# A two-layer hybrid decoder trunk: the last gate item behind the first half's branches, the first half's merged rows turned by VectorE and transfers, and a value product moved

## The chip, the core and the metric

The kernel runs on one core of a Trainium2 chip. The time is the device time of one execution in microseconds (us). Engines are TensorE (PE), VectorE (DVE), ScalarE (ACT), GpSimd (POOL) and the queue of SyncE (SP), which issues the transfers.

## What is computed

For each of two layers, on x of 256 rows and 1024 columns in float32 (cut from the reference):

```python
h = rms_norm(x)
proj = h @ w_in                    # pool | diff q,k,v | stick-breaking | forgetting | 4 x 1024 gate logits
gates = sigmoid(g_logit.reshape(b, s, 4, 1024) + b_gate)
merged = 0
for n, o in enumerate((o_pool, o_diff, o_sb, o_fox)):
    merged = merged + gates[:, :, n] * (o @ w_branch[rows of branch n])
x = x + merged @ w_out
x = x + swiglu(rms_norm(x))
```

The differential attention (four heads) and the forgetting attention, "fox" (four heads, taken as two pairs), are softmax attentions: scores, softmax, then probabilities times values.

## The kernel before

**Work and its units.** All weight matrices are streamed once per layer. A list `ITEMS` (L48 to L69) cuts them into items of 512 columns, and `plan_units` cuts the items into 144 units per layer, each of two blocks of 128 rows of the weights. An item's result is 2 x 128 rows by 512 columns and lies in one half of the PSUM tensor `bulk`; items take the two halves in turn, so an item may start only when the item two before it has been read out (`released_by`). Each weight is split into a rounded high part and the rest (`w_hi` by ScalarE, `w_lo` by VectorE), and so is each left operand; one block is three products (L1761, L1762, L1765), so a unit is 12 products of 512 columns (2 blocks x 2 row tiles x 3).

**Order of the items in a layer.** Seven items of the mixers (units 0 to 27), eight of the gates (28 to 59), then for each half j of the columns the four branches (1, 2, 1 and 1 units: 60 to 64 and 65 to 69), then `out` (70 to 77), then the feed-forward items from 78 on. Gate item g holds the logits of branch g // 2, half g % 2.

**The order around the items** is written out by hand. Each engine has a table from a slot to stages: TensorE's `MIXING_PE` says what it does ahead of unit "slot", `MIXING_ACT` and `MIXING_DVE` what ScalarE and VectorE do in their turn of the loop over units. In each turn these two run the slot's stages in the order of the table and then prepare the weights four units ahead (`split_hi`, L812, and `split_lo`, L1087). `split_hi` waits until the unit five before its own is done, which ties both engines to TensorE. VectorE's products of a branch (`branch`, L1388, gate times result) come after the table's stages of the same slot. Every engine works in order: what waits holds what is behind it.

**Attention stages.** For a head h: `scores` (TensorE, into banks A and B), `maxima` (VectorE, L1302 to L1305), `softmax` (exponentials by ScalarE, L968 to L970; scaling by VectorE), `tr_probs` (TensorE turns the probabilities, bank T, L1673), `probs_evac` (ScalarE copies them, `probsT`, L976), `pv` (TensorE, value product into bank O, L1683 to L1685) and `pv_evac` (VectorE copies it to `o_d`, L1338). Before TensorE writes a bank it waits for the last reader of that bank, in `take`:

```python
def pv(layer, kind, h):
    pe.wait_ge(probsT_ready, nth(probsT_ready, layer, (kind, h)))
    if kind == "diff":
        pe.wait_ge(v_ready, nth(v_ready, layer, ("dv", 1)))
        take("O", o_d_ready, layer, h)
```

**Turning rows.** Left operands must lie turned. The merged rows are turned by TensorE (`tr_merged`, L1703, four transposes for each row tile) into banks A and B for the first half and T and O for the second, then split by ScalarE (L816) and VectorE (L1094). The fox rows, the differential rows and the feed-forward activations go another way: VectorE transposes 32 x 32 blocks (`turn_blocks`, L1419) and transfers put the blocks in place, for the first two by way of DRAM (`rows_to_dram`, `rows_from_dram`), for the activations from SBUF to SBUF in four groups of four transfers (L690). SP issues such a group behind the weight load of its unit, and loads the weights six units ahead, each when its buffer is free.

**Merging.** GpSimd adds the four gated branches of a half (L784, six additions a half), in place in `wide`, once VectorE's products are there (`gated`), and signals `merged_ready`.

## Time and profile before

| | |
|---|---|
| median of 3 runs | 849.31 us (849.13 to 849.34) |
| the profiled execution | 849.36 us, its span 847.6 us |
| TensorE busy | 842.3 us (99%) |
| VectorE busy | 605.3 us (71%) |
| ScalarE busy | 445.5 us (53%) |
| GpSimd busy | 114.9 us (14%) |

A busy share is an average over the whole span. The timeline gives each instruction's start and length; in the chain of waits each piece is what the piece behind it waited for. "sb" and "wide" are SBUF tensors, "bank..." and "bulk" lie in PSUM.

### The profile page before, as it was taken

The numbers are of one execution on the slowest core, as the hardware profiler recorded it, in microseconds if no ns is written. First come the engines' busy times: TensorE is split into PE (matmuls) and PEld (weight loads), VectorE is DVE, ScalarE is ACT, GpSimd is POOL, SyncE is SP. The second block draws the span as 40 slices with busy tenths as digits, with TensorE's granted clock in tenths as the row PEclk, the third lists the DMA queues.
The fourth block names the chain that finished last, engine by engine and source line by source line (L and its number), as shares of the span: only waits on it lengthen the run. The fifth ranks groups of instructions, "written<-read, shape, count | busy, mean of one in ns | idle before, by whom it ended". The sixth has DMA issues, their size and how long they took to land.

```text
span 847.6 us, 11122 instructions
## 1 busy us (share of the span) xinstructions
PE 842.3 (99%) x4126; PEld 699.2 (83%) x4126; DVE 605.3 (71%) x890; ACT 445.5 (53%) x650; POOL 114.9 (14%) x89
## 2 busy tenths in 40 slices
PE   9999999999999999999999999999999999999998
PEld 7888888888888888888888888888888888888887
DVE  7885977679677666665479668868687776666643
ACT  6657645754454455444365675557543644444431
POOL 0750201004502000000005402010054000000000
PEclk9999999999999999999999999999999999999999
DMA  9846666477567777666566365764965577666651
GB/s 340 286 164 179 200 214 192 148 243 232 184 199 244 203 220 218 202 218 217 173 185 191 109 191 172 237 202 123 296 189 169 177 236 205 205 202 220 222 188 50
DMA packets 100934, 170.43 MB, mean 201 GB/s; under 512 B 12944, under 2 KB 26768, under 8 KB 100880
## 3 DMA queue, kind: packets, MB, share of 16 engines
q1 hardware_dynamic: 100448, 169.07, 63.8%
q8 instruction: 33, 0.54, 0.3%
q10 hardware_dynamic: 432, 0.66, 0.3%
q14 instruction: 21, 0.17, 0.1%
HBM read 160.77 MB, written 3.15 MB: 193 GB/s over the span
## 4 chain that ended last, share of the span: by engine, by line
PE 99%; DMA 1%; ACT 0%; issue 0%; DVE 0%; ACTq 0%
PE bulk L1761 30%; PE bulk L1765 30%; PE bulk L1762 30%; PE bankAB L1526 2%; DMA raw<-in_w_in_dram 1%; PE bankT L1673 0%; PE bulk L1808 0%; PE bankAB L1662 0%; PE bulk L1789 0%; PE bankAB L1620 0%; PE bulk L1795 0%; PE bankAB L1535 0%; PE bankO L1631 0%; PE bankO L1683 0%; PE bankO L1691 0%; PE bankO L1685 0%
## 5 line engine op out<-in xcount | busy, mean ns | idle before, releaser
L1087 DVE TENSOR_TENSOR w_lo<-raw,w_hi 128x1024 fp32r<-128x1024 f32 (+1 forms) x288 | 360.2, 1268 | 116.9 <-ACT w_hi L812 114.4
L812 ACT ACTIVATE w_hi<-raw 128x1024 fp32r<-128x1024 f32 (+1 forms) x286 | 295.5, 1047 | 206.7 <-PE bulk L1765 202.6
L1761 PE MATMUL bulk<-w_hi,hT_hi 128*128 128x512 f32 (+1 forms) x880 | 342.8, 390 | 0.0
L1762 PE MATMUL bulk<-w_lo,hT_hi 128*128 128x512 f32 (+1 forms) x880 | 339.3, 386 | 0.0
L1765 PE MATMUL bulk<-w_hi,hT_lo 128*128 128x512 f32 (+1 forms) x880 | 336.3, 386 | 0.0
L1761 PEld LDWEIGHTS bulk<-w_hi,hT_hi 128*128 128x128 f32 x880 | 165.3, 188 | 33.1 <-issue 0.5
L1765 PEld LDWEIGHTS bulk<-w_hi,hT_lo 128*128 128x128 f32 x880 | 165.0, 188 | 33.3
L1762 PEld LDWEIGHTS bulk<-w_lo,hT_hi 128*128 128x128 f32 x880 | 165.4, 188 | 32.0
L1761 PE MATMUL bulk<-w_hi,aT_hi 128*128 128x512 f32 x174 | 67.8, 390 | 0.0
L1765 PE MATMUL bulk<-w_hi,aT_lo 128*128 128x512 f32 x174 | 67.7, 389 | 0.0
L1762 PE MATMUL bulk<-w_lo,aT_hi 128*128 128x512 f32 x174 | 67.7, 389 | 0.0
L784 POOL TENSOR_TENSOR wide<-wide 128x512 f32<-128x512 f32 x24 | 44.2, 1860 | 117.1 <-DVE wide L1388 116.6
L1094 DVE TENSOR_TENSOR aT_lo<-wide,aT_hi 128x512 fp32r<-128x512 f32 (+1 forms) x24 | 14.5, 644 | 38.4 <-ACT aT_hi L816 38.4
L750 POOL TENSOR_TENSOR wide<-wide,ropeA 128x512 f32<-128x512 f32 x8 | 13.4, 1679 | 198.0 <-DVE wide L1190 197.9
L1761 PEld LDWEIGHTS bulk<-w_hi,aT_hi 128*128 128x128 f32 x174 | 32.7, 188 | 6.8
L1765 PEld LDWEIGHTS bulk<-w_hi,aT_lo 128*128 128x128 f32 x174 | 32.7, 188 | 6.8
L1762 PEld LDWEIGHTS bulk<-w_lo,aT_hi 128*128 128x128 f32 x174 | 32.7, 188 | 6.7
L816 ACT ACTIVATE aT_hi<-wide 128x512 fp32r<-128x512 f32 (+1 forms) x24 | 13.0, 589 | 45.9 <-DMA wide<-wide 45.9
L1761 PE MATMUL bulk<-w_hi,oT_hi 128*128 128x512 f32 x80 | 31.3, 391 | 0.0
L1765 PE MATMUL bulk<-w_hi,oT_lo 128*128 128x512 f32 x80 | 31.1, 389 | 0.0
L1762 PE MATMUL bulk<-w_lo,oT_hi 128*128 128x512 f32 x80 | 31.1, 389 | 0.0
L1011 ACT ACTIVATE wide<-bulk,y_ffn 128x512 f32<-128x512 f32 (+1 forms) x24 | 14.3, 650 | 18.2 <-PE bulk L1765 16.0
(239 smaller groups left out, 715.6 us busy)
## 6 DMA issues: line engine op xcount, KB each, us to landing
raw<-in_w_in_dram SPq DMA_DIRECT2D x110, 512.0 KB, 4.5
raw<-in_w_ffn_up_dram SPq DMA_DIRECT2D x80, 512.0 KB, 4.1
raw<-in_w_ffn_down_dram SPq DMA_DIRECT2D x44, 512.0 KB, 3.6
raw<-in_w_branch_dram SPq DMA_DIRECT2D x20, 512.0 KB, 5.3
raw<-in_w_out_dram SPq DMA_DIRECT2D x16, 512.0 KB, 3.3
wide<-wide SPq DMA_DIRECT2D x160, 32.0 KB, 2.7
bias<-in_b_gate_dram SPq DMA_DIRECT2D x16, 256.0 KB, 4.9
raw<-in_w_ffn_up_dram SPq DMA_DIRECT2D x16, 256.0 KB, 3.4
```

The source lines that it names most:

```text
L750: pool.tensor_tensor(ta, x, ropeA[:, i, t:t + 1, :].broadcast_to([P, 8, HD]), ALU.mult)
L784: ins = pool.tensor_tensor(m, m, wide[:, t, n * D + j * NC:n * D + (j + 1) * NC], ALU.add)
L812: act.activation(w_hi[:, g % RING, :, 0:width], raw[:, g % RAW, :, 0:width], ACT.Copy).then_inc(hi_ready, 1)
L816: ins = act.activation(dst, src, ACT.Copy) if scale is None else act.activation(dst, src, ACT.Copy, scale=scale)
L1011: act.activation(ff_tmp(t, p, width), item_bank(layer, ITEM_AT[item], t)[:, 0:width], ACT.Sigmoid, scale=y_ffn[:, t:t + 1]).then_inc(ff_si ...
L1087: vec.tensor_tensor(w_lo[:, g % RING, :, 0:width], raw[:, g % RAW, :, 0:width], w_hi[:, g % RING, :, 0:width].bitcast(F32), ALU.subtract). ...
L1094: ins = vec.tensor_tensor(dst, src, high.bitcast(F32), ALU.subtract)
L1526: ins = pe.matmul(dst, a[a_part], b[b_part], start=start and a_part + b_part == 0, stop=stop and a_part == 1, skip_group_check=True)
L1761: pe.matmul(dst, hi, whi, start=(k == ks[0]), stop=False)
L1762: pe.matmul(dst, hi, wlo, start=False, stop=False)
L1765: ins = pe.matmul(dst, lo, whi, start=False, stop=(k == ks[-1] or g == DEPTH * U - 2 and i == 1 and t == 1))
```

## The change

- The item of gate 7 (the gate of branch 3, second half) stands behind the four branches of the first half. The units are now: gates 0 to 6 at 28 to 55, first half's branches at 56 to 60, gate 7 at 61 to 64, second half's branches at 65 to 69 as before.
- The sigmoid of branch 3 is taken in two halves (`sigmoid_last`).
- The first half's merged rows are no longer turned by TensorE: VectorE turns them (stage `turn` "merged", slot 63), sixteen transfers from SBUF to SBUF in the queue at units 67 to 70 put them in place, and the split reads them from there in slot 68. Before, it read the banks in slot 69. The differential rows are turned in slot 48 instead of 49.
- The value product of differential head 2 moves on TensorE from slot 39 to slot 42, ahead of the transposes of head 3; its copy by VectorE moves from slot 39 to slot 42. `tr_forget` and `forget_evac` move from slot 39 to 37.

```diff
@@ -59,10 +59,11 @@
     ("dv", "w_in", [(OFF["dv"], 512)], KD),
     ("pf", "w_in", [(OFF["u"], 256), (OFF["f"], 4)], KD),
 ]
-ITEMS += [(("gate", g), "w_in", [(OFF["gate"] + g * NC, NC)], KD) for g in range(8)]
+GATES = [(("gate", g), "w_in", [(OFF["gate"] + g * NC, NC)], KD) for g in range(8)]

 KB = [range(0, 2), range(2, 6), range(6, 8), range(8, 10)]
-ITEMS += [(("branch", j, n), "w_branch", [(j * NC, NC)], KB[n]) for j in range(2) for n in range(4)]
+ITEMS += GATES[:7] + [(("branch", 0, n), "w_branch", [(0, NC)], KB[n]) for n in range(4)]
+ITEMS += GATES[7:] + [(("branch", 1, n), "w_branch", [(NC, NC)], KB[n]) for n in range(4)]
 ITEMS += [(("out", j), "w_out", [(j * NC, NC)], KD) for j in range(2)]
 NPAIR = 5
 for _p in range(NPAIR):
@@ -133,10 +134,10 @@
...
-    (37, "scores", "diff", 3), (37, "pv", "diff", 1), (39, "tr_probs", "diff", 2), (39, "pv", "diff", 2), (39, "tr_forget"), (42, "tr_probs", "diff", 3), (42, "scores", "fox", 0), (42, "pv", "diff", 3),
-    (52, "tr_probs", "fox", 1), (56, "pv", "fox", 1), (68, "tr_merged", 0),
-    (73, "tr_merged", 1)]
+    (37, "scores", "diff", 3), (37, "pv", "diff", 1), (37, "tr_forget"), (39, "tr_probs", "diff", 2), (42, "pv", "diff", 2),
+    (42, "tr_probs", "diff", 3), (42, "scores", "fox", 0), (42, "pv", "diff", 3), (47, "tr_probs", "fox", 0),
+    (56, "pv", "fox", 1), (73, "tr_merged", 1)]
...
@@ -173,7 +174,7 @@
     if stage == "pv":
         return [((stage, *args), "O")]
     if stage == "tr_merged":
-        return [((stage, args[0], t), ("AB", "TO")[args[0]][t]) for t in range(TT)]
+        return [((stage, args[0], t), "TO"[t]) for t in range(TT)]
     raise ValueError(stage)


@@ -189,9 +190,12 @@
 FF_BLOCKS = [4] * NPAIR + [2]
 FF_DONE = [FIRST[("ffu", _p)] + 4 for _p in range(NPAIR)] + [LAST["fflast"] + 1]
 FF_TURN = [_u + 1 for _u in FF_DONE[:-1]] + [FF_DONE[-1] + 4]
-TURN_AT = {"fox": 33, "diff": 49}
+TURN_AT = {"fox": 33, "diff": 48, "merged": 63}
 SPREAD_AT = {}
 BY_DRAM = ('fox', 'diff')
+for _s in ('merged',):
+    for _a in range(NQUAD):
+        SPREAD_AT.setdefault(TURN_AT[_s] + AHEAD + _a, []).append((_s, _a))
 for _s in ('fox', 'diff'):
     for _a, _way in enumerate(("out", "back")):
         SPREAD_AT.setdefault(TURN_AT[_s] + AHEAD + _a, []).append((_s, _way))
@@ -210,13 +214,13 @@
...
-    (36, "softmax", "diff", 2), (37, "probs_evac", "diff", 1), (38, "softmax", "diff", 3), (38, "probs_evac", "diff", 2),
+    (36, "softmax", "diff", 2), (37, "probs_evac", "diff", 1), (37, "forget_evac"), (38, "softmax", "diff", 3),
-    (55, "diff_evac", 0), (56, "pv_evac", "fox", 1), (60, "sigmoid", 3, 0), (61, "sigmoid", 3, 1), (69, "merged_evac", 0),
+    (49, "pool_evac_b"), (52, "probs_evac", "fox", 1), (53, "sigmoid", 2, 0), (53, "sigmoid", 2, 1), (55, "diff_evac", 1),
+    (55, "diff_evac", 0), (56, "pv_evac", "fox", 1), (57, "sigmoid_last", 0, 0), (57, "sigmoid_last", 0, 1),
+    (65, "sigmoid_last", 1, 0), (66, "sigmoid_last", 1, 1), (68, "merged_evac", 0), (72, "merged_evac", 1)]
...
@@ -225,11 +229,11 @@
...
-    (39, "pv_evac", "diff", 2), (39, "softmax", "diff", 3), (39, "fox_evac", "fq"), (39, "fox_evac", "fk"), (40, "gate", 2),
-    (41, "maxima", "fox", 0), (41, "softmax", "fox", 0), (42, "pv_evac", "diff", 3), (44, "gate", 3), (47, "maxima", "fox", 1),
-    (48, "diff_norm"), (48, "pv_evac", "fox", 0), (49, "softmax", "fox", 1), (49, "gate", 4), (49, "pool_evac_b"),
-    (49, "turn", "diff"), (52, "gate", 5), (55, "diff_evac", 1), (55, "diff_evac", 0), (56, "gate", 6),
-    (57, "pv_evac", "fox", 1), (60, "gate", 7), (69, "merged_evac", 0), (71, "merged_evac", 1)]
+    (39, "softmax", "diff", 3), (39, "fox_evac", "fq"), (39, "fox_evac", "fk"), (40, "gate", 2), (41, "maxima", "fox", 0),
+    (41, "softmax", "fox", 0), (42, "pv_evac", "diff", 2), (42, "pv_evac", "diff", 3), (44, "gate", 3),
+    (47, "maxima", "fox", 1), (48, "diff_norm"), (48, "pv_evac", "fox", 0), (48, "turn", "diff"), (49, "softmax", "fox", 1),
+    (49, "gate", 4), (49, "pool_evac_b"), (52, "gate", 5), (55, "diff_evac", 1), (55, "diff_evac", 0), (56, "gate", 6),
+    (57, "pv_evac", "fox", 1), (63, "turn", "merged"), (65, "gate", 7), (68, "merged_evac", 0), (71, "merged_evac", 1)]
...
@@ -457,7 +461,7 @@

             kind = stage if isinstance(stage, str) else stage[0]
             blocks = FF_BLOCKS[stage[1]] if kind == "act" else 4
-            return (*{"act": normed_place, "dq": late, "diff": late}.get(kind, early), blocks)
+            return (*{"act": normed_place, "diff": late, "merged": late}.get(kind, early), blocks)

         def spread_columns(stage, t, blocks):

@@ -545,7 +549,7 @@
         lam_exp = signal("lam_exp", ["exp"])
         lam_sum = signal("lam_sum", ["sum", "lam"])
         gate_ready = signal("gate_ready", [(g, t) for g in range(8) for t in range(TT)])
-        gate_open = signal("gate_open", [(n, t) for n in range(4) for t in range(TT)])
+        gate_open = signal("gate_open", [(n, t) for n in range(3) for t in range(TT)] + [(3, j, t) for j in range(2) for t in range(TT)])
         gated = signal("gated", [(j, n, t) for j in range(2) for n in range(4) for t in range(TT)])
         summed = signal("summed", [(j, n) for j in range(2) for n in (1, 2)])
         merged_ready = signal("merged_ready", [(j, t) for j in range(2) for t in range(TT)])
@@ -992,11 +996,21 @@
                 g = wide[:, t, n * D:(n + 1) * D]
                 act.activation(g, g, ACT.Sigmoid).then_inc(gate_open, 1)

+            def sigmoid_last(layer, j, t):
+                act.wait_ge(gate_ready, nth(gate_ready, layer, (6 + j, t)))
+                g = wide[:, t, 3 * D + j * NC:3 * D + (j + 1) * NC]
+                act.activation(g, g, ACT.Sigmoid).then_inc(gate_open, 1)
+
             def merged_evac(layer, j):
+                if j == 0:
+                    wait_spread(act, layer, "merged")
+                    for t in range(TT):
+                        lhs_part(layer, ("merged", 0, t), by_quads(hT[0], (0, 4), t), spread_columns("merged", t, (0, 4)))
+                    return
                 for t in range(TT):
                     act.wait_ge(stage_done, nth(stage_done, layer, ("tr_merged", j, t)))
                     lhs_part(layer, ("merged", j, t), hT[0][:, 4 * j:4 * j + 4, t * P:(t + 1) * P],
-                             bank[("AB", "TO")[j][t]].rearrange("p (k q) -> p k q", k=4))
+                             bank["TO"[t]].rearrange("p (k q) -> p k q", k=4))

             def ff_gate(layer, p):
                 item, width = (("ffg", p), NC) if p < NPAIR else ("fflast", 256)
@@ -1383,14 +1397,18 @@

                 for t in range(TT):
                     wait_item(vec, layer, ("branch", j, n), t)
-                    vec.wait_ge(gate_open, nth(gate_open, layer, (n, t)))
+                    vec.wait_ge(gate_open, nth(gate_open, layer, (n, t) if n < 3 else (n, j, t)))
                     g = wide[:, t, n * D + j * NC:n * D + (j + 1) * NC]
                     vec.tensor_tensor(g, item_bank(layer, ITEM_AT[("branch", j, n)], t), g, ALU.mult).then_inc(gated, 1)

             def merged_evac(layer, j):
                 for t in range(TT):
+                    if j == 0:
+                        lhs_rest(layer, ("merged", 0, t), by_quads(hT[1], (0, 4), t), spread_columns("merged", t, (0, 4)),
+                                 by_quads(hT[0], (0, 4), t))
+                        continue
                     lhs_rest(layer, ("merged", j, t), hT[1][:, 4 * j:4 * j + 4, t * P:(t + 1) * P],
-                             bank[("AB", "TO")[j][t]].rearrange("p (k q) -> p k q", k=4),
+                             bank["TO"[t]].rearrange("p (k q) -> p k q", k=4),
                              hT[0][:, 4 * j:4 * j + 4, t * P:(t + 1) * P])

             def ff_gate(layer, p):
@@ -1426,6 +1444,8 @@
                     turn_blocks(layer, stage, *(rotated, ("fk", 1)), lambda t: fox_gained[:, t, :])
                 elif stage == "diff":
                     turn_blocks(layer, stage, *(o_normed, "normed"), lambda t: o_d[:, t, :, :].rearrange("p h d -> p (h d)"))
+                elif stage == "merged":
+                    turn_blocks(layer, stage, *(merged_ready, (0, 1)), lambda t: merged(t)[:, 0:NC])

             def act_turn(layer, p):

@@ -1697,7 +1717,7 @@
             def tr_merged(layer, j):
                 for t in range(TT):
                     pe.wait_ge(merged_ready, nth(merged_ready, layer, (j, t)))
-                    name = ("AB", "TO")[j][t]
+                    name = "TO"[t]
                     take(name, lhs_lo, layer, ("merged", j, t))
                     for k in range(4):
                         ins = pe.transpose(bank[name][:, k * P:(k + 1) * P], merged(t)[:, (4 * j + k) * P:(4 * j + k + 1) * P], identity)
```


**TensorE, slot 39 before.** Transposes of head 2's probabilities, its value product (L1683 to L1685), and the transposes of the forget rows (L1554):

```order
L1673 MATMUL bankT<-con,probs_diff 128x128 [waits probsT_ready,probs_ready]
L1673 MATMUL bankT<-con,probs_diff 128x128 x2
L1683 MATMUL bankO<-v_d,probsT 128x128 [waits o_d_ready,v_ready,probsT_ready]
L1684 MATMUL bankO<-v_d,probsT 128x128
L1685 MATMUL bankO<-v_d,probsT 128x128
L1554 MATMUL bankT<-con,forget_rows 128x128 [waits probsT_ready,forget_out]
L1554 MATMUL bankT<-con,forget_rows 128x128 x3
```

The last two pieces leave this slot: the forget rows go to slot 37, the value product to slot 42, which now begins with it, head 3's transposes and the fox scores (lines of the changed file stand 20 further on):

```order
L1703 MATMUL bankO<-v_d,probsT 128x128 [waits o_d_ready,v_ready,probsT_ready]
L1704 MATMUL bankO<-v_d,probsT 128x128
L1705 MATMUL bankO<-v_d,probsT 128x128
L1693 MATMUL bankT<-con,probs_diff 128x128 [waits probsT_ready,probs_ready]
L1693 MATMUL bankT<-con,probs_diff 128x128 x2
L1546 MATMUL bankAB<-keys_hi,queries_hi 128x256 [waits forgetsT_ready,exped,qkT_ready,masks_ready]
L1546 MATMUL bankAB<-keys_hi,queries_hi 128x256
```

and ends with the last scores and head 3's value product, which waits for `o_d_ready`, as it did:

```order
L1674 MATMUL bankAB<-keys_hi,queries_hi 128x256 x2
L1677 MATMUL bankAB<-keys_hi,queries_hi 128x128 x2
L1682 MATMUL bankAB<-masks 128x256 x2
L1703 MATMUL bankO<-v_d,probsT 128x128 [waits o_d_ready,v_ready,probsT_ready]
L1704 MATMUL bankO<-v_d,probsT 128x128
L1705 MATMUL bankO<-v_d,probsT 128x128
```

Slot 42 so holds two value products into bank O, where it held one.

**VectorE, slots 41 and 42.** Before: the fox maxima and softmax, the low part for unit 45, one copy of a value product (head 3's):

```order
L1087 TENSOR_TENSOR w_lo<-raw,w_hi 128x1024 [waits hi_ready]
L1302 TENSOR_REDUCE row_max<-bankAB 128x2 [waits stage_done]
L1303 TENSOR_REDUCE row_max<-bankAB 128x2
L1305 TENSOR_SCALAR nmx<-row_max 128x4 [waits vec_step]
L1315 RECIPROCAL inverse<-den 128x4 [waits stage_done,exped]
L1330 TENSOR_SCALAR sb<-sb,inverse 128x256 [waits vec_step]
L1331 TENSOR_SCALAR sb<-sb,inverse 128x128
L1330 TENSOR_SCALAR sb<-sb,inverse 128x256
L1331 TENSOR_SCALAR sb<-sb,inverse 128x128
L1087 TENSOR_TENSOR w_lo<-raw,w_hi 128x1024 [waits hi_ready]
L1338 COPY o_d<-bankO 128x2x128 [waits stage_done]
```

In the change the same rows end with both copies, head 2's and head 3's, in one place (lines 14 further on); the copy of head 2 stood in slot 39, ahead of head 3's softmax:

```order
L1329 RECIPROCAL inverse<-den 128x4 [waits stage_done,exped]
L1344 TENSOR_SCALAR sb<-sb,inverse 128x256 [waits vec_step]
L1345 TENSOR_SCALAR sb<-sb,inverse 128x128
L1344 TENSOR_SCALAR sb<-sb,inverse 128x256
L1345 TENSOR_SCALAR sb<-sb,inverse 128x128
L1101 TENSOR_TENSOR w_lo<-raw,w_hi 128x1024 [waits hi_ready]
L1352 COPY o_d<-bankO 128x2x128 [waits stage_done] x2
L1101 TENSOR_TENSOR w_lo<-raw,w_hi 128x1024 [waits hi_ready] x2
```

So the copy of head 2's product has moved behind the fox maxima, the fox softmax and one low part.

**VectorE, slots 68 and 69.** Before, from the low parts of units 70 and 71: the product of branch 1 of the second half (slot 68), and behind it the split of the first half's merged rows out of bankAB (slot 69):

```order
L1087 TENSOR_TENSOR w_lo<-raw,w_hi 128x1024 [waits hi_ready] x2
L1388 TENSOR_TENSOR wide<-bulk,wide 128x512 [waits gate_open,unit_done] x2
L1087 TENSOR_TENSOR w_lo<-raw,w_hi 128x1024 [waits hi_ready]
L1094 TENSOR_TENSOR hT_lo<-bankAB,hT_hi 128x4x128 [waits lhs_hi] x2
L1388 TENSOR_TENSOR wide<-bulk,wide 128x512 [waits gate_open,unit_done] x2
L1087 TENSOR_TENSOR w_lo<-raw,w_hi 128x1024 [waits hi_ready]
```

Now, from gate 7 in slot 65: the split, out of the turned rows in `o_d`, stands in slot 68 ahead of that product:

```order
L1392 SCALAR_TENSOR_TENSOR wide<-bulk,y_attn,bias 128x512 [waits bias_loaded1,unit_done] x2
L1101 TENSOR_TENSOR w_lo<-raw,w_hi 128x1024 [waits hi_ready]
L1402 TENSOR_TENSOR wide<-bulk,wide 128x512 [waits gate_open,unit_done] x2
L1101 TENSOR_TENSOR w_lo<-raw,w_hi 128x1024 [waits hi_ready] x2
L1108 TENSOR_TENSOR hT_lo<-o_d,hT_hi 128x4x128 [waits lhs_hi] x2
L1402 TENSOR_TENSOR wide<-bulk,wide 128x512 [waits gate_open,unit_done] x2
L1101 TENSOR_TENSOR w_lo<-raw,w_hi 128x1024 [waits hi_ready]
```

The split has changed places with the product of branch 1.

## Rows read from the trace of the kernel before

**Rows 1.** The page: busy time of TensorE, its granted clock by slice, the chain's shares.
```profile
PE 842.3 (99%) x4126; PEld 699.2 (83%) x4126; DVE 605.3 (71%) x890; ACT 445.5 (53%) x650; POOL 114.9 (14%) x89
...
PEclk9999999999999999999999999999999999999999
...
PE 99%; DMA 1%; ACT 0%; issue 0%; DVE 0%; ACTq 0%
```

**Rows 2.** Who waited for whom, TensorE: us in total, times, longest.
```profile
PE bankO L1683 <- ACT probsT L976: 1.2, 2, 0.6
```

**Rows 3.** Timeline, slot 39, layer 0: start us, us, engine line operation.
```profile
123.51 0.49 PE L1673 MATMUL bankT<-con,probs_diff 128*128 128x128 f32 x3
...
124.03 0.49 ACT L976 ACTIVATE probsT<-bankT 128x384 f32<-128x384 f32 x1
...
124.58 0.49 PE L1683 MATMUL bankO<-v_d,probsT 128*128 128x128 f32 x2 [0.58 <-ACT probsT L976]
```

**Rows 4.** The chain of waits, layer 0, units 56 to 68: start us, us, what.
```profile
181.41 0.43 PE bulk L1761
...
214.32 0.87 PE bankAB L1703 x8
```

**Rows 5.** Timeline, slot 42, layer 0, TensorE, VectorE and ScalarE.
```profile
135.85 0.39 PE L1683 MATMUL bankO<-v_d,probsT 128*128 128x128 f32 x2
...
136.05 0.69 DVE L1302 TENSOR_REDUCE row_max<-bankAB 128x2 f32<-128x512 f32 x1 [2.35 <-PE bankAB L1662]
...
137.31 0.48 ACT L968 ACTIVATE sb<-bankAB,nmx 128x256 f32<-128x256 f32 x1 [1.36 <-DVE nmx L1305]
...
139.06 0.18 DVE L1315 RECIPROCAL inverse<-den 128x4 f32<-128x4 f32 x1 [1.79 <-ACT sb L970]
...
140.20 1.22 DVE L1087 TENSOR_TENSOR w_lo<-raw,w_hi 128x1024 fp32r<-128x1024 f32 x1
...
141.34 0.42 DVE L1338 COPY o_d<-bankO 128x256 f32<-128x256 f32 x1
```

**Rows 6.** Timeline, layer 0, first half's branch 1 and the additions behind it.
```profile
200.75 1.29 DVE L1388 TENSOR_TENSOR wide<-bulk,wide 128x512 f32<-128x512 f32 x2 [0.34 <-PE bulk L1765]
...
201.52 11.69 POOL L784 TENSOR_TENSOR wide<-wide 128x512 f32<-128x512 f32 x6 [55.59 <-DVE wide L1388]
```

**Rows 7.** Timeline, feed-forward part: turns, transfers and copies of two activation tiles.
```profile
269.54 1.29 DVE L1419 STREAM_TRANSPOSE wide<-wide 128x512 f32<-128x512 f32 x2
...
272.54 2.50 SPq L690 DMA_DIRECT2D wide<-wide  x4
...
281.87 3.20 SPq L690 DMA_DIRECT2D wide<-wide  x4
...
286.34 1.16 ACT L816 ACTIVATE aT_hi<-wide 128x512 fp32r<-128x512 f32 x2 [1.90 <-DMA wide<-wide]
...
287.00 1.29 DVE L1094 TENSOR_TENSOR aT_lo<-wide,aT_hi 128x512 fp32r<-128x512 f32 x2 [1.30 <-ACT aT_hi L816]
...
292.07 1.30 DVE L1419 STREAM_TRANSPOSE wide<-wide 128x512 f32<-128x512 f32 x2
...
308.17 1.16 ACT L816 ACTIVATE aT_hi<-wide 128x512 fp32r<-128x512 f32 x2 [1.97 <-DMA wide<-wide]
```

**Rows 8.** Timeline, layer 0: the turn and the landing of the differential rows.
```profile
162.04 0.42 DVE L1094 TENSOR_TENSOR oT_lo<-bankO,oT_hi 128x256 fp32r<-128x256 f32 x1 [0.88 <-ACT oT_hi L816]
...
167.36 1.29 DVE L1419 STREAM_TRANSPOSE v_d<-o_d 128x512 f32<-128x512 f32 x2
...
182.32 1.34 ACT L816 ACTIVATE oT_hi<-o_d,small 128x512 fp32r<-128x512 f32 x2 [5.03 <-DMA o_d<-rows_diff]
...
183.08 2.19 DVE L1363 SCALAR_TENSOR_TENSOR oT_lo<-o_d,small,oT_hi 128x128 fp32r<-128x128 f32 x8 [4.35 <-ACT oT_hi L816]
```

**Rows 9.** Timeline, start of the kernel: the warm-up products.
```profile
0.97 4.63 PE L1817 MATMUL bulk<-warm 128*128 128x128 bf16 x48 [0.97 <-DVE warm L1452]
...
4.83 0.78 PE L1817 MATMUL bulk<-warm 128*128 128x128 bf16 x11
```

More of the change, by code:

```diff
@@ L135 @@
     (30, "scores", "diff", 1), (30, "pv", "diff", 0), (35, "cum"), (35, "scores", "diff", 2), (35, "tr_probs", "diff", 1),
-    (37, "scores", "diff", 3), (37, "pv", "diff", 1), (39, "tr_probs", "diff", 2), (39, "pv", "diff", 2), (39, "tr_forget"), (42, "tr_probs", "diff", 3), (42, "scores", "fox", 0), (42, "pv", "diff", 3),
-    (47, "tr_probs", "fox", 0), (47, "scores", "fox", 1), (47, "pool_a"), (47, "pv", "fox", 0), (50, "pool_b"),
-    (52, "tr_probs", "fox", 1), (56, "pv", "fox", 1), (68, "tr_merged", 0),
-    (73, "tr_merged", 1)]
+    (37, "scores", "diff", 3), (37, "pv", "diff", 1), (37, "tr_forget"), (39, "tr_probs", "diff", 2), (42, "pv", "diff", 2),
+    (42, "tr_probs", "diff", 3), (42, "scores", "fox", 0), (42, "pv", "diff", 3), (47, "tr_probs", "fox", 0),
+    (47, "scores", "fox", 1), (47, "pool_a"), (47, "pv", "fox", 0), (50, "pool_b"), (52, "tr_probs", "fox", 1),
+    (56, "pv", "fox", 1), (73, "tr_merged", 1)]
 _PE = [(0, "tr_norm", "attn", 0, 1)] + MIXING_PE + [(F0, "tr_norm", "ffn", 0, 1)]
@@ L1029, in _ @@
                           diff_evac=diff_evac, gate=nothing, sigmoid=sigmoid, branch=nothing,
-                          merged_evac=merged_evac, ff_gate=ff_gate, ff_up=nothing, turn=nothing, act_turn=nothing, act_evac=act_evac)
+                          merged_evac=merged_evac, ff_gate=ff_gate, ff_up=nothing, sigmoid_last=sigmoid_last, turn=nothing, act_turn=nothing, act_evac=act_evac)
             def first_hi(k):
```

4 lines of the change are left out of this document (1 added, 3 removed).

## The prediction

> **What bounds the kernel now.** I read the page first: TensorE is busy for 842.3 of 847.6 us, and the chain of waits lies on it for 99% [rows 1]. So the time is TensorE's own work plus whatever it stands still for, and the table of who waited for whom is short: apart from the start it has one line, two waits for the turned probabilities, 1.2 us in total [rows 2]. VectorE, ScalarE, GpSimd and the queues have slack on average, but the average says nothing about one place. A change of order can win only what TensorE no longer does or waits for; it can lose as much as any single wait it makes. So after the gains I follow each piece that was moved, with its queue, in the timeline.
>
> One unit of weights (12 products) takes TensorE 2.7425 us: unit 56 starts at 181.41, slot 68 at 214.32, nothing but 12 units between them [rows 4]. The start of unit k in the timeline of before is 181.41 + (k - 56) x 2.7425. Everything is worked out for layer 0 on this time base and doubled, since both layers run the same order.
>
> **Gains.** (a) The eight transposes of the first merged half leave TensorE: 0.87 us in the chain [rows 4], per layer. Twice: -1.7. (b) In slot 39 the value product of the third differential head follows its own transposes at once and waits for ScalarE's copy. The three transposes start at 123.51, take about 0.11 apart, and something else could start at 123.84; the product starts at 124.58 [rows 3]. So 0.74 us, twice -1.5 (the table's 1.2 counts from the modelled end of the transposes). In slot 42 that copy is long done. The product itself and the four transposes of the forget rows are only moved. In slot 37 ScalarE now stands before the forget copy until TensorE has come there; the hi part queued behind it is used by VectorE some us later, so I cost that at nothing. The split last sigmoid is ScalarE work beside TensorE's, at nothing too.
>
> **First new wait, slot 42.** TensorE now does: value product 2, transposes 3, scores of the first fox pair, value product 3. Both value products write bank O, so product 3 waits until VectorE has copied product 2 out. That copy used to be in VectorE's slot 39; it now stands in slot 42, behind the fox maxima, the fox softmax and a w_lo part of slot 41 (front matter, VectorE's order). And the fox maxima wait for the scores that TensorE issues just ahead of product 3. So TensorE waits for a whole round trip that begins with its own scores. The trace has this trip, since the copy of product 3 stood at its end: maxima from 136.05, ScalarE's exponentials from 137.31, VectorE again from 139.06, the w_lo part at 140.20, the copy 141.34 to 141.76; TensorE issued product 3 at 135.85 [rows 5]. 141.76 - 135.85 = 5.91, and 0.05 for the hand-over (ScalarE ends at 124.52, TensorE starts at 124.58 [rows 3]). I take 5.96, twice +11.9. Nothing in the trip depends on what was moved, so I give it 5.5 to 6.3. What queues behind the wait is every later product of TensorE; the other engines only get ahead, and I count no gain for that.
>
> **Second new wait, unit 69.** The branches of the first half now lie four units earlier. VectorE's product of branch 1 came right after unit 62, which ended at 200.61, and GpSimd's six additions ran from 201.52 for 11.69 us, to 213.21 [rows 6]. Four units earlier is 10.97 us earlier: merged rows complete at 202.24, VectorE turns them then. From there I take the price of the same thing in the feed-forward part, with the same sixteen 32 KB transfers and four weight loads between them: VectorE's turn at 269.54, transfers issued from 272.54 to 285.07 (the last group 281.87 + 3.20), ScalarE's copy at 286.34, VectorE's subtractions 287.00 to 288.29; a second time 292.07 to 308.17 [rows 7]. So 16.1 to 16.8 us from turn to ScalarE's copy: 218.3 to 219.0, and 1.95 more until both subtractions are done: 220.3 to 221.0. In slot 68 VectorE's order has these subtractions ahead of the product of branch 1 of the second half, which is what frees the bank for the second half's branch 3, unit 69. Its first tile takes half of 1.29 [rows 6]: 220.9 to 221.6, and the hand-over. Unit 69 would start at 181.41 + 13 x 2.7425 = 217.06. Wait: 3.9 to 4.6, I take 4.3, twice +8.6. Before, nothing stood ahead of that product. The bounds are wider than these two samples: 3 if the queue of transfers, free of feed-forward traffic, lands each group sooner; 6 if GpSimd or the turn is late by a unit's half.
>
> **What stays hidden.** The differential rows are needed at unit 57 (184.15) instead of 61. Before, VectorE was through with them at 185.27 (183.08 + 2.19), 1.1 late for the new order; but their turn moves from 167.36 to right behind the fox copy that ends at 162.46 [rows 8], 4.9 earlier, and their way out one load earlier in the queue. 3.8 to spare: nothing, at most the 1.1 and a gate product behind it. The 16 added transfers hold the queue for some 0.6 us each, and the weight loads behind them run six units ahead of their use: nothing. The last transposes (slot 73) follow a POOL chain that the second wait shifts by as much as TensorE: 0 to 0.5.
>
> Sum without the clock: 849.36 (the profiled execution; the median of the runs is 849.31) - 1.7 - 1.5 + 11.9 + 8.6 = **866.7 us**.
>
> **The clock.** The 48 warm-up products of 128 columns took 4.44 us, from 0.97 to 5.41, against 48 x 0.057 = 2.7 at the pace of the units (2.7425 / 12 / 4); the last 11 lie clearly closer (0.78 us) than the rest [rows 9]. So TensorE, idle before the kernel, begins at the lower level (1.2 GHz) though the column of the granted clock prints 1.00 there, and to climb once costs 1.7 us. No row shows whether 6 us of standing still bring it back; after the start it never stood for more than 0.6 us [rows 2]. Bounds are nothing and 1.7 for each of four waits, 0 to +6.8. I take it for the two long ones and not for the two shorter: +3.4.
>
> The Trainium skill, page "TensorE: Matmul & The Clock Gate", Part 1, says that the throttled level is the default and that activity releases it, and warns against gaps between bursts of products. By that page all four waits may bring the clock down (the third rival); the start of this trace agrees with its first half, no row here bears on the second.
>
> **Forecast: 870.1 us**, 2.4% slower. 0.44.
>
> **Rivals.**
> - The clock holds: 866.7. For it: every slice of the page has the clock at full, across all the small waits [rows 1]. 0.13.
> - The clock falls at all four waits: 866.7 + 6.8 = 873.5. 0.13.
> - Only the first wait is there, since the transfers land over 4 us sooner than the feed-forward ones: 849.4 - 3.2 + 11.9 = 858.1, 861.5 with the clock. Against it: the queue issues its four groups one weight load apart, which sets 12 of the 16 us. 0.11.
> - Only the second: 854.8. It needs the copy of product 2 ahead of the fox maxima, and the order has it behind. 0.04.
> - A third wait: the differential rows land late at unit 57, or GpSimd's last additions hold the transposes of slot 73, 1 to 3.5 us per layer: 872 to 877. For it: ScalarE stood 5.0 us for this very transfer before [rows 8]. 0.10.
> - **Not slower.** Place: bank O in slot 42 and the bank of unit 69. If VectorE stands far enough ahead at both (5.96 and 4.3 us), TensorE keeps only the gains, 849.4 - 3.2 = 846.1. It decides when both waits together fall below 1.6 us per layer, the gains. Against it: the first trip starts with TensorE's own scores, so no lead of VectorE's shortens it. 0.05.
>
> **How the numbers follow.** The range reaches from the first wait alone with the clock's price (861.5, less 1.5 for the spread of its terms) to the upper end of a third wait: 860 to 877. Outside are "only the second", "not slower", the first wait alone at full clock and what lies above 877, about 0.15. Faster by over 0.2% (what a measurement of this kernel can tell from no change): 0.05. Within 0.2%: 0.01. Slower: 0.94.
>
> **What would show it.** TensorE's waits: a new line at the first value product of a differential head for VectorE's copy of o_d, some 5.8 us, twice; a new line at a bulk product for VectorE's wide, about 4 us, twice; the 1.2 us for probsT gone, the eight transposes into bankAB gone. Busy TensorE falls in share, not in us, unless the granted clock shows slices below 1 after the waits. ScalarE's first-half copy starts 16 to 17 us after the turn. Wrong would be: no wait at bank O (my reading of the order fails), a turn long before 202 on this time base, or a wait at unit 57.

## The result and the profile after

| | before | after |
|---|---|---|
| median | 849.22 us (848.98 to 849.34, 4 runs) | 877.12 us (875.34 to 877.60, 4 runs) |
| the profiled execution | 849.36 us, span 847.6 us | 875.34 us, span 873.5 us |

The change is slower: ratio 1.0325, interval 1.0307 to 1.0343. The page of the kernel after, the lines that answer to [rows 1] (granted clock by slice, in tenths, and the chain's shares):

```profile
PE 849.1 (97%) x4110; PEld 703.9 (81%) x4110; DVE 607.7 (70%) x894; ACT 445.7 (51%) x654; POOL 112.2 (13%) x89
...
PEclk9999998999899999999999999989998999999999
...
PE 95%; DVE 2%; DMA 1%; ACT 1%; SPq 1%; issue 1%; ACTq 0%; DVEq 0%
```

TensorE has 16 instructions less and is busy 6.8 us longer: the granted clock is below full in four slices. The chain of waits leaves TensorE for 5% of the span. Who was waited for, against [rows 2] (us in total, times, longest):

```profile
PE bankO L1703 <- DVE o_d L1352: 11.8, 2, 5.9
PE bulk L1781 <- DVE wide L1402: 8.7, 2, 4.8
```

The wait for probsT is gone, and there are two new lines, each twice. These are the two waits that the prediction named.

**Slot 42**, timeline of layer 0 (start us, us, engine line operation), against [rows 5]:

```profile
134.44 0.39 PE L1682 MATMUL bankAB<-masks 128*128 128x256 bf16 x2
...
134.87 0.69 DVE L1316 TENSOR_REDUCE row_max<-bankAB 128x2 f32<-128x512 f32 x1 [1.38 <-PE bankAB L1682]
...
136.13 0.47 ACT L972 ACTIVATE sb<-bankAB,nmx 128x256 f32<-128x256 f32 x1 [1.36 <-DVE nmx L1319]
...
139.02 1.22 DVE L1101 TENSOR_TENSOR w_lo<-raw,w_hi 128x1024 fp32r<-128x1024 f32 x1
140.15 0.42 DVE L1352 COPY o_d<-bankO 128x256 f32<-128x256 f32 x1
...
140.72 0.77 PE L1703 MATMUL bankO<-v_d,probsT 128*128 128x128 f32 x2 [5.88 <-DVE o_d L1352]
```

The round trip is the one read in the trace of before: scores, maxima at 134.87, exponentials at 136.13, a w_lo part at 139.02, the copy of product 2 at 140.15. The masks' two products end their turn at about 134.67; the value product starts at 140.72, 6.05 us later.

**Unit 69**, layer 0, against [rows 6, 7]:

```profile
197.32 11.57 POOL L788 TENSOR_TENSOR wide<-wide 128x512 f32<-128x512 f32 x6 [51.50 <-DVE wide L1402]
```
```profile
208.94 1.30 DVE L1437 STREAM_TRANSPOSE v_d<-wide 128x512 f32<-128x512 f32 x2 [1.19 <-POOL wide L788]
...
226.48 1.29 DVE L1108 TENSOR_TENSOR hT_lo<-o_d,hT_hi 128x512 fp32r<-128x512 f32 x2 [5.79 <-ACT hT_hi L820]
227.69 1.28 DVE L1402 TENSOR_TENSOR wide<-bulk,wide 128x512 f32<-128x512 f32 x2
```
```profile
211.79 3.41 SPq L694 DMA_DIRECT2D o_d<-v_d  x4
...
215.87 2.42 SPq L694 DMA_DIRECT2D o_d<-v_d  x4
...
218.97 2.41 SPq L694 DMA_DIRECT2D o_d<-v_d  x4
...
222.04 2.41 SPq L694 DMA_DIRECT2D o_d<-v_d  x4
```
```profile
225.82 1.15 ACT L820 ACTIVATE hT_hi<-o_d 128x512 fp32r<-128x512 f32 x2 [6.39 <-DMA o_d<-v_d]
```
```profile
228.52 0.77 PE L1781 MATMUL bulk<-w_hi,oT_hi 128*128 128x512 f32 x1 [4.81 <-DVE wide L1402]
...
661.03 0.77 PE L1781 MATMUL bulk<-w_hi,oT_hi 128*128 128x512 f32 x1 [3.90 <-DVE wide L1402]
```

From VectorE's turn to ScalarE's copy it is 16.88 us, and VectorE's subtraction stands ahead of the branch product that frees the bank. The last product before the wait started at 223.33, so the next was due at 223.56 and came at 228.52: 4.96 us. In layer 1 the idle time shown is 3.90; from start to start, counted in the same way, it is 4.06 (656.74 to 661.03, less the 0.23 of one product).

**The clock**, TensorE in three stretches around the first wait (stretch: us, busy (instructions), granted clock, DMA share, GB/s):

```profile
134.80:140.70 5.90, 0.03 (x1) 0.74 0.39 126
140.70:144.30 3.60, 3.58 (x12) 0.50 0.50 148
144.30:148.00 3.70, 3.70 (x17) 0.98 0.47 142
```

After the wait the granted clock is 0.50, the lower of the two levels (1.2 GHz), for 3.6 us, and the bulk products lie 0.427 us apart; then they lie 0.2275 apart. The same shows behind all four waits, for 3.6 and 4.4 us in layer 0, 3.9 and 5.7 in layer 1. A product of 0.427 us loses 0.20, a share of 0.467: 17.6 x 0.467 = 8.2 us. With it the profiled execution adds up: 849.36 - 3.2 (the gains as predicted) + 2 x 6.05 + 4.96 + 4.06 + 8.2 = 875.5, against 875.34.

The differential rows came in time for unit 57: VectorE's split ran from 185.04, behind 0.77 of waiting, and TensorE's table has no line for it.

### The profile page after: what moved, and what is told of

Read it like the earlier page. It is cut to its first block, busy times and chain, and to the rows that moved or that the text cites. A ratio compares the mean times of both kernels' runs of the same rounds, so it can differ in the third digit from the quotient of the medians.

```text
span 873.5 us, 11126 instructions
## 1 busy us (share of the span) xinstructions
PE 849.1 (97%) x4110; PEld 703.9 (81%) x4110; DVE 607.7 (70%) x894; ACT 445.7 (51%) x654; POOL 112.2 (13%) x89
## 4 chain that ended last, share of the span: by engine, by line
PE 95%; DVE 2%; DMA 1%; ACT 1%; SPq 1%; issue 1%; ACTq 0%; DVEq 0%
PE bulk L1781 29%; PE bulk L1782 29%; PE bulk L1785 29%; PE bankAB L1546 2%; SPq L694 1%; DMA raw<-in_w_in_dram 1%; DVE w_lo L1101 1%; PE bankT L1693 0%; PE bankAB L1682 0%; PE bulk L1828 0%; DMA o_d<-v_d 0%; PE bulk L1809 0%; PE bankAB L1640 0%; PE bulk L1815 0%; PE bankO L1703 0%
## 5 line engine op out<-in xcount | busy, mean ns | idle before, releaser
L1781 PE MATMUL bulk<-w_hi,oT_hi 128*128 128x512 f32 x80 | 33.6, 420 | 8.7 <-DVE wide L1402 8.7
L1782 PE MATMUL bulk<-w_lo,oT_hi 128*128 128x512 f32 x80 | 33.0, 412 | 0.0
L1781 PEld LDWEIGHTS bulk<-w_hi,oT_hi 128*128 128x128 f32 x80 | 16.1, 201 | 13.2 <-issue 9.8
```

Of the source, the lines that this page charges most:

```text
L1781: pe.matmul(dst, hi, whi, start=(k == ks[0]), stop=False)
L1782: pe.matmul(dst, hi, wlo, start=False, stop=False)
```

## The experiments

**Undo the first wait** (e1): VectorE copies product 2 one slot earlier, ahead of the fox maxima.

```diff
-... (41, "maxima", "fox", 0),
-    (41, "softmax", "fox", 0), (42, "pv_evac", "diff", 2), (42, "pv_evac", "diff", 3), ...
+... (41, "pv_evac", "diff", 2), (41, "maxima", "fox", 0),
+    (41, "softmax", "fox", 0), (42, "pv_evac", "diff", 3), ...
```

> The changed kernel with one entry moved: VectorE copies the third differential head's product in slot 41, ahead of the fox maxima, instead of in slot 42. Theory (both waits are real and each lowers the clock): the 5.9 us wait of TensorE at bank O goes in both layers and with it the stretches at half clock behind it (3.7 and 3.9 us of work, so 1.7 and 1.8 us lost): 877.1 - 12.0 - 3.5 = 861.6 us, TensorE's second wait stays at about 4.9 and 3.8 us. Rival (the copy only looks like the cause, and TensorE is held by something else in slot 42, such as the probabilities or bank A and B): the wait stays with another releaser, above 873 us.

Measured 858.41 us (858.13 to 858.61), ratio 1.0108 (1.0093 to 1.0123). Only the second line was left:

```profile
PE bulk L1781 <- DVE wide L1402: 8.6, 2, 4.7
```

Taking away two waits of 6.05 us gave 18.7 us, 6.6 more than the waits themselves. Between the profiled executions it is 17.2 (875.34 to 858.13), and that adds up: 12.1 of waits, 3.5 of the low stretches behind them, which go with them, and 1.4 because the two stretches that stay are 4.0 and 3.1 us long instead of 4.4 and 5.7, and cost 3.3 together instead of 4.7. So the expected 861.6 was 3.2 too high: 1.4 of that is the shorter stretches, and 1.8 that the median of the change lies above its profiled execution.

**Undo the second wait, first try** (e2): VectorE's split of the merged rows one slot later, behind the branch product.

```diff
-    ... (65, "gate", 7), (68, "merged_evac", 0), ...
+    ... (65, "gate", 7), (69, "merged_evac", 0), ...
```

> The changed kernel with one entry moved: VectorE splits the first merged half in slot 69, behind the product of branch 1 of the second half, instead of in slot 68. Theory: unit 69 no longer waits; unit 70 then waits for the split itself and for the branch product behind it, about 1.8 us, too short for the clock: 877.1 - 8.7 + 3.6 - 4.5 (clock) = 867.5 us, 865 to 869. Rival (the transfers' landing alone sets the time, wherever the split stands): the wait only moves to unit 70 and keeps 4 us or more per layer, above 874 us.

Measured 875.28 us (875.01 to 876.42), ratio 1.0312 (1.0294 to 1.0329), 1.8 below the change, and the two intervals overlap: next to none of the 9.6 us expected. The timeline of e2, VectorE and TensorE in layer 0:

```profile
221.51 1.29 DVE L1402 TENSOR_TENSOR wide<-bulk,wide 128x512 f32<-128x512 f32 x2 [0.34 <-PE bulk L1785]
228.29 1.23 DVE L1101 TENSOR_TENSOR w_lo<-raw,w_hi 128x1024 fp32r<-128x1024 f32 x1 [5.49 <-ACT w_hi L816]
229.43 1.29 DVE L1108 TENSOR_TENSOR hT_lo<-o_d,hT_hi 128x512 fp32r<-128x512 f32 x2
230.63 1.28 DVE L1402 TENSOR_TENSOR wide<-bulk,wide 128x512 f32<-128x512 f32 x2
```
```profile
231.42 0.77 PE L1781 MATMUL bulk<-w_hi,hT_hi 128*128 128x512 f32 x1 [4.51 <-DVE wide L1402]
```

The branch product at 221.51 no longer waits, but the next w_lo part waits 5.49 us for ScalarE, whose high part is stuck behind its own copy of the merged rows (started at 226.16). The wait moved one unit on. So both engines hold their queues for the transfers.

**Both moves together** (e4), the edits of e1 and e2.

> The moves of the first two experiments together. Theory: gains 3.2 us in two layers (eight transposes each, 1.7; the wait for the probabilities, 1.5), one wait of about 1.8 us left per layer at unit 70, no slice below full clock: 849.2 - 3.2 + 3.6 = 849.6 us, 848.5 to 850.5. Rival (the new places of the items cost something the two waits hid, at unit 57 or slot 73): above 851 us, with a third wait in the table.

Measured 858.86 us (858.57 to 859.01), ratio 1.0113 (1.0098 to 1.0128), the same as e1 within 0.5, and not the 849.6 expected: the second move is worth nothing with the first wait gone, either. The line of waits reads like that of e1, though the wait now stands ahead of unit 70, as in e2 (beside it there is one wait of 0.7 us in the feed-forward part of layer 1):

```profile
PE bulk L1781 <- DVE wide L1402: 8.8, 2, 4.8
```

**The waits with TensorE kept busy** (e3): 100 idle products of 128 columns into an unused part of bank T stand ahead of the value product of head 3. What the kernel computes is unchanged.

```diff
+                if (kind, h) == ("diff", 3):
+                    for _ in range(100):
+                        pe.matmul(bank["T"][:, 384:512], warm[:, :], warm[:, :], start=True, stop=True)
```

> The changed kernel with 100 idle products of TensorE (zeros into unused columns of bank T) put ahead of the value product of head 3 in both layers, inside the wait; they change no result. At the pace of full clock they fill about 5.7 of the 6.0 us. Theory (standing still lowers the clock): product 3 starts at the same time, the granted clock stays at 1.0 behind the first wait, 1.7 and 1.8 us come back: 877.1 - 3.5 = 873.6 us. Rival (what is lost behind the wait is not the clock, or idle products do not hold it): 877 us, the same slices below 1.

Measured 871.98 us (871.24 to 872.17), ratio 1.0267 (1.0251 to 1.0282), 5.1 below the change. Its second wait, and TensorE in layer 0:

```profile
PE bulk L1784 <- DVE wide L1402: 9.3, 2, 5.4
```
```profile
134.83 5.75 PE L1700 MATMUL bankT<-warm 128*128 128x128 bf16 x100
140.88 0.46 PE L1706 MATMUL bankO<-v_d,probsT 128*128 128x128 f32 x2 [0.30 <-DVE o_d L1352]
```

The value product comes as late as before, 6.05 us after the end of the masks' products, and no low stretch follows it. The waits did not get shorter, so the time is won by the clock alone, but not all of it behind the first waits. Between the profiled executions it is 4.1 us (875.34 to 871.24): 3.5 behind the first waits, as expected, and 1.3 because the stretches behind the second waits are 4.0 and 3.4 us long here instead of 4.4 and 5.7, less 0.6 for second waits that are longer (5.55 and 4.09 us from start to start). The rest of the 5.1 comes from the medians, which lie 1.8 (the change) and 0.7 (e3) above the profiled executions.

**Idle products in both waits** (e11): as e3, and 66 more ahead of unit 69.

> The changed kernel with idle products of TensorE in both waits (100 ahead of head 3's value product, 66 ahead of unit 69); nothing else is changed. Theory (waits and clock are all there is): no slice below full clock, 849.2 - 3.2 + 12.0 + 8.7 = 866.7 us, plus what the waits measured between starts add, up to 868. Rival (the clock costs less than the 8 to 10 us that are unexplained by the waits): above 870 us with the clock at full.

Measured 869.82 us (869.78 to 871.42), ratio 1.0234 (1.0211 to 1.0257), 7.3 below the change. Its waits:

```profile
PE bulk L1790 <- DVE wide L1404: 3.4, 2, 2.1
...
PE bankO L1708 <- DVE o_d L1354: 0.6, 2, 0.3
```

It is above the 866.7 to 868 expected, and just below the 870 of the rival. I had filled the second wait by its length in the change, but here it is longer. In layer 0 the idle products start at 222.17 and the next unit at 228.18, 6.01 us instead of 4.96; in layer 1 654.33 to 659.48, 5.15. The turn to ScalarE's copy took 17.91 us (207.56 to 225.47); the first group of transfers took 4.55 us where the change has 3.41. Why that group is slower was not tried. With the waits as they were, the expectation's own sum gives 849.2 - 3.2 + 12.1 + 11.2 = 869.3, so waits and clock are enough and the rival falls. In the profiled execution, 871.42, one low stretch of 3.4 us follows the 2.14 us left unfilled in layer 0; the three others ran at a granted clock of 1.000, at 869.8, and they are 1.6 us shorter, which is the price of such a stretch (3.4 x 0.467). With the waits of the profiled execution put in for theirs, their sum is 849.31 + 2 x 6.05 + 6.01 + 5.15 - 869.8 = 2.8 us of gains. That is a low count, since small pieces beside the waits are left out, 0.18 us ahead of unit 70 in layer 1 for one (662.07 to 662.48). The same sum over the profiled executions of the change, e1 and e3 gives 3.3 to 3.4.

**Only the value product** (e6): the kernel before, with product 2 in slot 42, the forget transposes in 37, and VectorE's copy ahead of the fox maxima.

```diff
-    ... (39, "tr_probs", "diff", 2), (39, "pv", "diff", 2), (39, "tr_forget"), (42, "tr_probs", "diff", 3), ...
+    ... (37, "tr_forget"), (39, "tr_probs", "diff", 2), (42, "pv", "diff", 2), (42, "tr_probs", "diff", 3), ...
```

> The kernel before with one piece of the change alone: the third head's value product in slot 42, the forget rows in slot 37, and VectorE's copy in slot 41 ahead of the fox maxima. Theory: the two waits of 0.58 us for the probabilities go, 0.74 us from start to start: 849.2 - 1.5 = 847.7 us, no line of waits left after the start. Rival (the wait is hidden or comes back as another, by the copy's new place or by ScalarE standing before the forget copy in slot 37): 849.2 us.

Measured 847.51 us beside 849.22, ratio 0.9985 (0.9977 to 0.9993). The start is the only wait left:

```profile
PE bulk L1817 <- DVE warm L1452: 1.0, 1, 1.0
```

**The new order of items, rows still turned by TensorE** (e7): e6's moves, the last gate item behind the first half's branches, the split last sigmoid, and the eight transposes kept in slot 68 with the splits in 69.

> As the run before, with the new order of the items as well (gate 7 behind the first half's branches), but the first merged half turned by TensorE in slot 68, as before. Theory: the order of the items by itself costs and gives nothing: 847.7 us, no wait at units 57, 61, 66 or 69. Rival (it tightens unit 57, where the differential rows are now due, or a bank of the gates): a wait of 1 us or more there, above 849 us.

Measured 847.45 us, ratio 0.9980 (0.9972 to 0.9989), the same as e6: the order of the items costs and gives nothing, and there is no wait at units 57, 61, 66 or 69. The eight transposes are in it, with no wait on either side:

```profile
213.25 1.03 PE L1714 MATMUL bankAB<-con,wide 128*128 128x128 f32 x8
214.04 0.48 PE L1772 MATMUL bulk<-w_hi,oT_hi 128*128 128x512 f32 x1
```

They hold TensorE for 0.79 us, and the product behind 214.04 starts at 214.36, 0.09 later than at the usual pace: 0.88 us in a layer.

**The splits behind everything** (e9): the change with the copy first, ScalarE's and VectorE's splits in slot 69, and VectorE's branch products ahead of the table's stages in a slot.

```diff
-    (65, "sigmoid_last", 1, 0), (66, "sigmoid_last", 1, 1), (68, "merged_evac", 0), (72, "merged_evac", 1)]
+    (65, "sigmoid_last", 1, 0), (66, "sigmoid_last", 1, 1), (69, "merged_evac", 0), (72, "merged_evac", 1)]
...
-    return sorted(norms + mixing + list(branches) + ffn, key=lambda e: e[0])
+    return sorted(norms + list(branches) + mixing + ffn, key=lambda e: e[0])
```

> The change with the copy first, and the split of the first merged half put where neither the branch products nor the low part of unit 72 stand behind it: ScalarE's copy and VectorE's subtraction both in slot 69, branch products ahead of a slot's other stages. Theory (what made the second wait was what stood behind the landing, and the landing itself is nearly in time): ScalarE copies at about 218.1 in layer 0, the split is done 1.3 us later, unit 70 waits 0.5 to 1.5 us: 849.2 - 3.2 + 2 = 848.0 us, 847 to 849.5, the clock at full. Rival (the landing alone sets it): 3 us or more at unit 70, above 852 us.

Measured 850.77 us (849.93 to 852.60), ratio 1.0023 (1.0012 to 1.0033), above the 847 to 849.5 expected and below the 852 of the rival: most of the second wait is gone, and what is left is for the split rows themselves, which are ready only behind the start that unit 70 would have:

```profile
PE bulk L1781 <- DVE hT_lo L1108: 3.9, 3, 2.2
```
```profile
219.27 2.26 DVE L1108 TENSOR_TENSOR hT_lo<-o_d,hT_hi 128x512 fp32r<-128x512 f32 x2 [1.44 <-ACT hT_hi L820]
```
```profile
214.26 6.12 POOL L788 TENSOR_TENSOR wide<-wide 128x512 f32<-128x512 f32 x4 [12.90 <-DVE wide L1402]
```

The subtraction takes 2.26 us for two tiles, against 1.29 in the change (3.37 in layer 1, where the wait is 0.97 and 0.77 us, one for each tile). Until 220.4 it runs beside GpSimd's additions of the second half, which in the change begin only behind it.

**Fewer and shorter issues, by way of DRAM** (e5): e9, and the merged rows go out in one transfer and come back in four.

```diff
-BY_DRAM = ('fox', 'diff')
-for _s in ('merged',):
-    for _a in range(NQUAD):
-        SPREAD_AT.setdefault(TURN_AT[_s] + AHEAD + _a, []).append((_s, _a))
-for _s in ('fox', 'diff'):
+BY_DRAM = ('fox', 'diff', 'merged')
+for _s in ('fox', 'diff', 'merged'):
```

> As the run before, with the merged rows put in place by way of DRAM (one transfer out, four back) instead of sixteen from SBUF to SBUF. Theory (the queue's sixteen issues, 2.4 us a group and one weight load between, set the landing): it lands about 1.5 us sooner, nothing is left to wait for: 849.2 - 3.2 = 846.0 us, 845.5 to 847, faster than the kernel before by 0.4%. Rival (the way out and back takes longer than the issues, 6.8 and 5.3 us for the differential rows before): unit 70 waits as in the run before or longer, 848 us or more.

Measured 847.55 us, ratio 0.9981 (0.9973 to 0.9990), 3.2 below e9. It falls between the two cases: the rows come sooner, but unit 70 still waits for their split, which takes 2.38 us beside GpSimd's additions:

```profile
PE bulk L1778 <- DVE hT_lo L1105: 1.4, 2, 0.7
```

**DRAM alone** (e10): the change with the copy first and the way by DRAM; the splits stay in slot 68.

> The change with VectorE's copy first (slot 41) and the merged rows put in place by way of DRAM; the split stays where the change has it, slot 68, ahead of the branch product. Theory (with this way the rows land by 214.3, a unit before they are split; the 0.7 us left in the run before came from GpSimd slowing the subtraction, 2.4 us for two tiles instead of 1.3, in slot 69): split at about 214 to 215.3, the branch product is in time for unit 69, no wait at all: 849.2 - 3.2 = 846.0 us, 845.7 to 846.4. Rival (the landing is later than ScalarE's copy showed, or the subtraction is as slow in slot 68): a wait of 0.5 to 1 us at unit 69, 847.0 to 848.5.

Measured 848.01 us (847.68 to 848.41), ratio 0.9981 (0.9972 to 0.9990), with the waits

```profile
PE bulk L1778 <- DVE wide L1399: 1.0, 2, 0.8
```

and the queue and ScalarE's copy in layer 0:

```profile
204.02 0.47 SPq L581 DMA_DIRECT2D rows_merged<-v_d  x1
...
209.78 1.75 SPq L588 DMA_DIRECT2D o_d<-rows_merged  x4
```
```profile
214.00 1.16 ACT L817 ACTIVATE hT_hi<-o_d 128x512 fp32r<-128x512 f32 x2 [2.35 <-DMA o_d<-rows_merged]
```

The turn was at 201.17, so turn to copy is 12.8 us instead of 16.9. The rows went out and back, and still came earlier: what was long was the row of sixteen issues with weight loads between them, not the way of the data. (This way has also fewer transfers, five for sixteen; the two were not tried apart.) Against the 846.0 expected, 2 us are missing. The median lies 0.3 above the profiled execution, and that one, 847.68, has the other 1.7 as waits, more than the table says if one counts from start to start: 0.93 and 0.39 us ahead of unit 69 and 0.18 in each layer ahead of unit 70, for which the table has no line. The subtraction took 1.29 us, so it was not what the rival feared; a wait at unit 69 there was, as the rival said.

**The same transfers from two queues** (e8): the change with the copy first; groups 2 and 3 are issued by ScalarE in slots 64 and 65.

```diff
+            def issue(layer, a):
+                turned, spread, blocks = turning("merged")
+                act.wait_ge(block_turned, nth(block_turned, layer, "merged"))
+                for b in range(NQUAD):
+                    act.dma_start(spread[b * QUAD:(b + 1) * QUAD, a, :, 0:blocks, :], ...).then_inc(block_spread, 16)
```

> The change with the copy first, and two of the four groups of transfers issued by ScalarE's queue (slots 64 and 65), two by SP's; places of the split as in the change. Theory (the issues set the landing): the last group of SP is out at about 210.7 instead of 216.8, the rows are there before slot 68, no wait at unit 69: 846.0 us, up to 847. Rival (the transfers share the 16 engines with the weight loads and land late whoever issues them, or ScalarE's issues hold up its weight parts): a wait of 1 us or more, above 848 us.

Measured 847.60 us (847.47 to 848.10), ratio 0.9977 (0.9968 to 0.9986). This is above the 847 expected and below the 848 of the rival. ScalarE's queue and copy, layer 0:

```profile
202.63 2.52 ACTq L1003 DMA_DIRECT2D o_d<-v_d  x4
...
205.25 1.06 ACT L816 ACTIVATE w_hi<-raw 128x1024 fp32r<-128x1024 f32 x1 [4.35 <-PE bulk L1792]
205.27 2.46 ACTq L1003 DMA_DIRECT2D o_d<-v_d  x4
...
212.46 1.14 ACT L820 ACTIVATE hT_hi<-o_d 128x512 fp32r<-128x512 f32 x2
```

Turn (201.29) to copy is 11.2 us with all sixteen transfers, and the copy and unit 69 wait no more. The table has another line instead:

```profile
PE bulk L1788 <- DVE wide L1399: 0.9, 2, 0.5
```
```profile
207.48 1.40 DVE L1399 SCALAR_TENSOR_TENSOR wide<-bulk,y_attn,bias 128x512 f32<-128x512 f32 x2
```

L1399 is here VectorE's reading out of gate 7, and it is unit 66 that waits for it. ScalarE's high part starts at 205.25, behind 4.35 us of standing that the issues fill; VectorE's low part waits 2.64 us for it, and the reading out of gate 7 stands behind that. This is the second half of the rival, ScalarE's issues holding up its weight parts.

## Why the prediction came out as it did

The median is 877.12, 0.1 us above the stated upper end; the profiled execution, 875.34, is inside. The sign and both places are right. Of the cases it is the clock falling at all four waits (873.5; the list of rivals has it second, though the paragraph on the clock calls it the third), not the forecast of 870.1, and the measured time lies above that case too. That the range reaches up to 877 comes from a third wait that is not there; that it comes so near to the measured time is luck. By its own steps:

- **Gain (b), the value product behind its transposes**, taken as 1.5: e6 has 1.7. Right.
- **Gain (a), the eight transposes**, taken as 1.7: no run had it alone, but the traces bear it out, with 0.88 us in a layer in e7. e5, e8 and e10, without the transposes, are no faster than e7 with them, because they have waits of nearly the same length in their place: from start to start 0.86 and 0.87 us in the two layers of e5, 1.11 and 0.57 in e10, 0.73 and 0.70 in e8. The gains of 3.2 fit the sums of the change, e1 and e3 (3.3 to 3.4).
- **First wait**, 5.96 each: 6.05 in both layers, and e1 shows that only the place of one copy makes it. Right.
- **Second wait**, 4.3 each: 4.96 and 4.06. Right within its bounds; the turn to the copy took 16.88 us where the feed-forward part had 16.1 to 16.8. What the prediction lacked was a second holder: it named VectorE's split as what holds the branch product, and e2 shows that ScalarE's copy holds the high parts as well, so that moving VectorE's split alone gives nothing. That cost no number of the prediction, but the expectations of e2 and e4.
- **The clock**, taken as +3.4: this is the term that failed. The step was "1.7 for the two long ones and not for the two shorter", with 6.8 as the upper bound. The stretches at half clock are 3.6 to 5.7 us long and cost 1.7, 2.1, 1.8 and 2.6 us, 8.2 together. So it was wrong twice: in which waits count, and in pricing each by the one rise at the start of the kernel [rows 9], which was taken as the upper bound of a fall and is near the lower end of what was measured (1.5 to 2.9 us over the change, e1, e2 and e4). Of the 5.2 us between 870.1 and the profiled execution, 4.8 are this term. e3 and e11 show it as cause: with TensorE kept busy in the waits, the time falls by 5.1 and 7.3 us though the waits stay as long or longer.
- **By the rule of the Trainium skill**, page "TensorE: Matmul & The Clock Gate", Part 1 (gaps between bursts of products bring the throttle back), all four waits could bring the clock down, and they did; the prediction named the rule and gave it 0.13. With no row that spoke against it, and a rule that spoke for it, that was too little.
- **Third wait at unit 57 or slot 73**: not there; ScalarE's copy of the differential rows waited 1.27 us, and no one behind it; e7, where no first wait delays TensorE, has no wait at unit 57 either.
- **Not slower**: reached by e5, e8 and e10, at 847.6 to 848.0, once the copy stands first and the rows are there 4 to 6 us sooner. The threshold of 1.6 us per layer fits what was run: at waits of 0.6 to 1.1 us per layer, from start to start, the gains show, and e9, with 2.4 and 2.1 us, is slower than the kernel before. Nothing between was tried.

The versions that beat both kernels are e6, e7, e5 and e8, within 0.15 us of each other, and e10, 0.4 to 0.6 behind them, all 0.15 to 0.23% below the kernel before. Of these e6 is the smallest edit. Turning the first half by VectorE and transfers adds nothing to it in any form that was run: the waits it makes take what the transposes give.

## What to carry to other kernels

When a product is moved behind other work, look at who last reads the bank it writes, and where that reader now stands in its own queue: here one copy behind a softmax cost 18.7 us, ten times what the move could win. Price a transfer that replaces transposes by the time its queue needs to issue it, and count every engine that copies or splits its result as holding its whole queue until it lands. And where TensorE is the bound, a wait of a few us costs its length and then a stretch at half clock, here 1.5 to 2.9 us more for each.

## What the runs showed that I had not expected

- The low stretch is not one size: 3.6, 4.4, 3.9 and 5.7 us behind waits of 6.05, 4.96, 6.05 and 4.06 us; in e1, behind the same second waits, 4.0 and 3.1. The longest wait did not have the longest stretch, and the median of the change lies 1.8 us above its fastest run. Its two slowest runs have a mean granted clock of 0.982 where the two others have 0.984, which speaks for longer stretches in them, but no trace of them shows it.
- A wait of 2.19 us in e9 was followed by a low stretch of 3.4 us, and one of 2.14 us in e11's profiled execution too, though e11's three other runs stayed at 1.000; waits of 0.97 (e9, layer 1) and 1.29 us (e11, layer 1) by none.
- VectorE's subtraction of SBUF rows beside GpSimd's additions takes 2.26 us (e9) or 2.38 (e5) where it takes 1.29 without them (the change, e8, e10).
- One transfer out to DRAM and four back are faster (12.8 us from turn to copy) than sixteen direct ones from one queue (16.9), and slower than the sixteen from two queues (11.2).
